# Setup, first norm and recurrence as one block; first mixture-of-experts layer, key norm and attention as another

## What is computed

```python
hn = rmsnorm(h, norm_mix_w[0])                       # layer 0: gated linear recurrence
q, f, i, g = split(hn @ w_in)
fg = lb + (1 - lb) * sigmoid(f); o, s = gla_chunked(silu(q), 1 - fg, i, log(fg), s0)
h = h + (rmsnorm(o, gnorm_w) * silu(g)) @ w_o
h = h + hier_moe(rmsnorm(h, norm_ffn_w[0]))          # 16 experts, 2 per token
kv = rmsnorm(h, kv_norm_w) @ w_kv                    # shared keys and values
hn = rmsnorm(h, norm_mix_w[1]); q = hn @ b_w_q       # layer 1: differential attention
h = h + (rmsnorm(attn(q, kv, cache), subln_w) * (1 - lam_init)) @ b_w_o
h = h + hier_moe(rmsnorm(h, norm_ffn_w[1])); y = rmsnorm(h, final_norm_w)
```

## Time and profile before

| | |
|---|---|
| median of three runs | 1624.22 us (1623.5 to 1628.1) |
| the profiled execution | 1626.92 us, its span 1625.2 us |
| PE busy | 1337.0 us (82%) |
| DVE busy | 745.8 us (46%) |
| ACT busy | 391.1 us (24%) |
| POOL busy | 168.7 us (10%) |
| granted PE clock, mean | 0.909 |

### The profile page before, as it was taken

One profiled execution on the slowest core, in us unless ns is written; L12 is line 12 of the kernel. 1 busy time (PEld: TensorE's weight loads), 2 busy tenths in 40 slices (PEclk: granted clock), 3 DMA queues, 4 the chain that ended last, 5 costly groups with the idle time before them and its releaser, 6 DMA issues. The chain is left out here.

```text
span 1625.2 us, 29095 instructions
## 1 busy us (share of the span) xinstructions
PE 1337.0 (82%) x11207; PEld 763.4 (47%) x11207; DVE 745.8 (46%) x1890; ACT 391.1 (24%) x1064; POOL 168.7 (10%) x242
## 2 busy tenths in 40 slices
PE   3999999988799998925999985877788589999880
PEld 2445555555456655513454542443444145765440
DVE  4315665656665311124110644787787166421115
ACT  2023443443110211103011022344444111121111
POOL 1002332332001000020000001001000001100002
PEclk9999999998898999966999988899898889799995
DMA  6141433123614999940132759999999761699924
GB/s 211 52 136 42 134 102 126 57 67 119 231 58 184 328 352 342 306 148 23 52 107 96 288 174 401 380 406 383 382 403 357 271 246 55 248 381 352 333 57 165
DMA packets 132156, 347.56 MB, mean 214 GB/s; under 512 B 22012, under 2 KB 51887, under 8 KB 123824
## 3 DMA queue, kind: packets, MB, share of 16 engines
q1 hardware_dynamic: 115652, 315.21, 53.7%
q0 software_dynamic: 4992, 17.83, 3.1%
q10 hardware_dynamic: 11372, 12.62, 2.5%
HBM read 302.09 MB, written 43.52 MB: 213 GB/s over the span
## 5 line engine op out<-in xcount | busy, mean ns | idle before, releaser
L404 PE MATMUL bank<-wring,xT 128*128 128x512 f32 x512 | 227.8, 602 | 5.0 <-PEq L359 4.4
L404 PEld LDWEIGHTS bank<-wring,xT 128*128 128x128 f32 x512 | 96.9, 192 | 124.6 <-issue 123.2
L785 PE MATMUL bank<-xT,wring 128*128 128x512 f32 x256 | 115.6, 609 | 10.2 <-DVE hgrn_g L621 10.2
L1313 PE MATMUL bank<-wring,xT 128*128 128x512 f32 x256 | 120.4, 624 | 2.0 <-DVE xT L1233 2.0
L2310 DVE STREAM_TRANSPOSE wring<-wring 128x1024 f32<-128x1024 f32 x64 | 77.2, 1227 | 41.8 <-DMA wring<-cache_k 41.5
L2310 DVE STREAM_TRANSPOSE attn_q_xT<-attn_q_xT 128x1024 f32<-128x1024 f32 x64 | 77.0, 1227 | 32.1 <-DMA attn_q_xT<-cache_k 31.8
L785 PEld LDWEIGHTS bank<-xT,wring 128*128 128x128 f32 x256 | 49.0, 194 | 73.3 <-issue 59.8
L1313 PEld LDWEIGHTS bank<-wring,xT 128*128 128x128 f32 x256 | 49.8, 201 | 60.1 <-issue 60.0
L695 DVE COPY_PREDICATED gla_att<-level_masks,bank 128x512 f32<-128x512 int32 x48 | 35.1, 731 | 61.3 <-PE bank L805 61.3
L1946 PE MATMUL bank<-attn_q_xT,wring 128*128 128x512 f32 x128 | 56.9, 597 | 0.0
L805 PE MATMUL bank<-gla_qe,gla_ke 128*128 128x128 f32 x384 | 51.8, 293 | 0.0
(11 more groups left out here) (426 smaller groups left out, 2329.7 us busy)
## 6 DMA issues: line engine op xcount, KB each, us to landing
wring<-cache_k SPq DMA_DIRECT2D x64, 512.0 KB, 7.1
attn_q_xT<-cache_k SPq DMA_DIRECT2D x64, 512.0 KB, 8.0
xT<-cache_v SPq DMA_DIRECT2D x60, 512.0 KB, 7.6
wring<-cache_v SPq DMA_DIRECT2D x56, 512.0 KB, 6.1
moe_wd<-moe_w_down SPq DMA_DIRECT2D x20, 1024.0 KB, 13.5
wring<-moe_w_gate SPq DMA_DIRECT2D x18, 1024.0 KB, 11.2
wring<-moe_w_up SPq DMA_DIRECT2D x18, 1024.0 KB, 14.1
wring<-a_w_in SPq DMA_DIRECT2D x16, 1024.0 KB, 8.6
```

Source lines behind the costliest of these rows:

```text
L404: last = nc.tensor.matmul(bank[:, :], xT[:, c, cols(t)], w[:, c, :], start=(c == 0), stop=(c == DC - 1))
L785: last = nc.tensor.matmul(bank[:, :], lhsT, k.xT[:, c, 0:SEQ], start=(c == 0), stop=(c == DC - 1))
L1313: last = nc.tensor.matmul(bank[:, :], k.xT[:, c, cols(t)], w[:, c, :], start=(c == 0), stop=(c == DC - 1))
```

## The change

The setup, the mix0 norm and the recurrence form one block; layer 0's output projection, experts, combination, the mix1 norm, projections and attention form another; layer 1's experts and the final combination form a third. Three blocks stand where there were nine.

In the first, SP issues the first three weight tiles right behind the tokens, without the waits for the small weights. ACT loads the column weights first, then the row weights. The norm goes by tile with `root` and `scale`; PE turns tiles 0 and 1, and then turns tile t + 2 behind value unit (0, t). DVE's clearing is spread between its copies. The lambda scalar is made later.

In the second, POOL waits for one semaphore (`finished`) that PE raises when all stores have landed, and gathers into ten buffers; `add` waits for both gathers of a tile; DVE adds, scales and turns out tile by tile, and PE projects both halves of the keys of tile t (four banks) as soon as its transposed tile is out. The second sample query goes from head 1 to head 4, and the spread of the sample queries from head 2 to head 6. The last expert's narrow stores are issued by SP and not by ACT, and the loop over extra blocks lies inside one `If(more > 0)`. In the third block the same holds, with six gather buffers for four. A small table load for the square root (`load_table`) stands ahead of the norms. Slot numbers and gates move to tiles that outlive the layer.

```diff
-            sp.wait_ge(columns_in, 16 * len(by_feature))
-            sp.wait_ge(rows_in, 16 * 6)
-            for i in range(2):
-                k.load_weights(sp, column_halves(a["a_w_in"][0], 2 * D + i * HB))
-            k.load_weights(sp, head_pair_halves(a, 0))
-            sp.wait_ge(tokens_in, 16 * NT)
...
+    def sync(self, sp):
+        k, a = self.k, self.a
+        for t in range(PT):
+            sp.dma_start(k.h[:, t, :], a["x_prompt"][0, t * P:(t + 1) * P, :]).then_inc(self.tokens_in[t], 16)
+        sp.dma_start(k.h[0:SMP, PT, :], a["x_sample"].rearrange("b t d -> (b t) d")).then_inc(self.tokens_in[PT], 16)
+        for i in range(2):
+            k.load_weights(sp, column_halves(a["a_w_in"][0], 2 * D + i * HB))
+        k.load_weights(sp, head_pair_halves(a, 0))
...
+    def scalar(self, act):
+        k, a = self.k, self.a
+        for i, w in enumerate(self.by_feature):
+            act.dma_start(self.weight_rows[i * DC:(i + 1) * DC, :], w.rearrange("(c p) -> c p", p=P)).then_inc(self.columns_in, 16)
+        act.dma_start(k.rowbuf[:, 0:P], a["a_gnorm_w"]).then_inc(self.rows_in, 16)
+        act.dma_start(k.rowbuf[:, P:2 * P], a["b_subln_w"]).then_inc(self.rows_in, 16)
+        for i, w in enumerate((a["b_lambda_q1"], a["b_lambda_k1"], a["b_lambda_q2"], a["b_lambda_k2"])):
+            act.dma_start(self.lam[:, i, :], w).then_inc(self.rows_in, 16)
...
+    def spread_rows(self, pe):
+        k, nc = self.k, self.nc
+        pe.wait_ge(self.rows_in, 16 * 6)
+        nc.tensor.matmul(k.ps[7][:, 0:2 * P], k.ones[0:1, :], k.rowbuf[:, 0:2 * P], start=True, stop=True).then_inc(self.spread, 1)
...
+                setup.scalar(act)
+                norm.root(act, 0)
+                for t in range(NT):
+                    if t + 1 < NT:
+                        if t + 1 == PT:
+                            act.wait_ge(setup.padded, 1)
+                        norm.root(act, t + 1)
+                    if t == 0:
+                        act.wait_ge(setup.out, 1)
+                    norm.out_second(act, t)
+                setup.lambda_exponentials(act)
...
+                setup.pad_rows(dve)
+                norm.scale(dve, ch, 0)
+                setup.lambda_products(dve)
+                setup.columns(dve)
+                dve.wait_ge(setup.out, 1)
+                norm.out_first(dve, 0)
+                norm.scale(dve, ch, 1)
+                norm.out_first(dve, 1)
+                norm.scale(dve, ch, 2)
+                setup.row_gains(dve)
+                norm.scale(dve, ch, 3)
+                norm.out_first(dve, 2)
+                norm.scale(dve, ch, 4)
+                value_out(0, 0)
+                norm.out_first(dve, 3)
+                nc.vector.memset(below[:, :, :], 0.0).then_inc(zero_made, 1)
+                value_out(0, 1)
+                norm.out_first(dve, 4)
+                bounds()
+                setup.lambda_sum(dve)
+                value_out(0, 2)
+                clear_level(0)
+                value_out(0, 3)
+                clear_level(1)
+                value_out(0, 4)
+                clear_level(2)
...
+                pe.wait_ge(setup.ident_made, 1)
+                norm.turn(pe, 0)
+                setup.turn_columns(pe)
+                norm.turn(pe, 1)
+                setup.spread_rows(pe)
+                w = k.take_weights(pe)
+                for t in range(NT):
+                    pe.wait_ge(norm.out_v, t + 1)
+                    pe.wait_ge(norm.out_a, t + 1)
+                    by_token(("v", 0, t), w)
+                    if t + 2 < NT:
+                        norm.turn(pe, t + 2)
+                k.w_done.append((proj_done, units[("v", 0, NT - 1)][0]))
+                w = k.take_weights(pe)
+                for t in range(NT):
+                    by_token(("v", 1, t), w)
+                    if t == 0:
+                        setup.spread_lambda(pe)
+                k.w_done.append((proj_done, units[("v", 1, NT - 1)][0]))
...
+        self.store_narrow(sp, E - 1, (E - 1) % NB, (E - 1) * CAP)
...
-        with sp.Fori(0, MORE) as i:
-            with sp.If(i < more):
+        with sp.If(more > 0):
+            with sp.Fori(0, MORE) as i:
...
-        pe.wait_ge(y_out[0], more * (16 * STORES) + 16 * STORES * loads_before(NB, 0))
+            pe.wait_ge(y_out[0], 16 * STORES * (loads_before(NB, 0) + MORE))
+        pe.wait_ge(y_out[0], 16 * STORES * loads_before(NB, 0))
         pe.wait_ge(y_out[1], 16 * STORES * loads_before(NB, 1))
...
+    def gpsimd(self, pool):
+        pool.wait_ge(self.finished, 1)
+        B = len(self.rows_in)
+        for n in range(TOPK * NT):
+            t, j = n // TOPK, n % TOPK
+            if n >= B:
+                pool.wait_ge(self.added, n - B + 1)
+            pool.indirect_dma_start(self.rows_in[n % B][0:rows(t), :], None, self.slots_y,
+                                    bass.IndirectOffsetOnAxis(ap=self.k.slot_i[0:rows(t), j, t:t + 1], axis=0))\
+                .then_inc(self.landed[n % B // TOPK], 16)
...
+    def add(self, dve, t):
+        k, B = self.k, len(self.rows_in)
+        for j in range(TOPK):
+            n = TOPK * t + j
+            if j == 0:
+                dve.wait_ge(self.landed[n % B // TOPK], 16 * TOPK * (n // B + 1))
+            if n:
+                dve.wait_ge(self.added, n)
+            part = k.h[0:rows(t), t, :]
+            self.nc.vector.scalar_tensor_tensor(out=part, in0=self.rows_in[n % B][0:rows(t), :], scalar=k.gates[0:rows(t), j, t:t + 1],
+                                                in1=part, op0=ALU.mult, op1=ALU.add).then_inc(self.added, 1)
...
+        k.w_done += [(self.k_done, 2 * NT - 1), (self.k_done, 2 * NT)]
+        self.norm.turn(pe, 0)
+        for n, (i, t) in enumerate(self.k_units):
+            if i == 0:
+                pe.wait_ge(self.norm.out_v, 2 * t + 1)
+                pe.wait_ge(self.norm.out_a, 2 * t + 1)
+            if n >= 4:
+                pe.wait_ge(self.k_out, n - 3)
+            project_tokens(nc, k.ps[n % 4], self.kv_xT, w[i], t).then_inc(self.k_done, 1)
+            if i == 0 and t + 1 < NT:
+                self.norm.turn(pe, t + 1)
...
+            if h == 4:
+                w.append(k.take_weights(pe))
+            if h % 4 == 0:
+                sample_q(h // 4, w[h // 4])
+            if h == 0:
+                pe.wait_ge(self.k_out, 2 * NT)
...
-            if h == 2:
+            if h == 6:
...
+        sp.wait_ge(self.combine.added, TOPK * NT)
...
+        def tile(t):
+            add(dve, t)
+            norm.scale(dve, ch, t)
+        tile(0)
+        norm.out_first(dve, 0)
+        tile(1)
+        tile(2)
+        norm.out_first(dve, 1)
+        key_out(0)
+        tile(3)
+        key_out(1)
+        norm.out_first(dve, 2)
+        key_out(2)
+        tile(4)
+        key_out(3)
+        norm.out_first(dve, 3)
+        key_out(4)
+        key_out(5)
+        norm.out_first(dve, 4)
+        for n in range(6, 2 * NT):
+            key_out(n)
...
+    def norm_scalar(self, act):
+        norm = self.norm
+        norm.load_table(act)
+        norm.root(act, 0)
+        norm.out_second(act, 0)
+        norm.root(act, 1)
+        for t in range(1, NT):
+            if t + 1 < NT:
+                norm.root(act, t + 1)
+            norm.out_second(act, t)
...
+                ffn.vector(dve)
+                ch = Chain(dve, k.order["vector"], k.order_n["vector"])
+                proj.combine_and_keys(dve, ch)
...
+            rows_in = [tile[:, t, :] for tile in (g, v) for t in range(NT)]
...
+                rows_in = [qo[:, t, :] for t in range(PT)] + [xs[:, PT, :], xs[:, PT - 1, :]]
```

528 lines of the change are left out of this document (251 added, 277 removed).

## The result

The changed kernel takes 1572.89 us (median of four runs, 1572.28 to 1574.52) against 1623.86 us before (four runs, 1617.76 to 1628.1); the ratio is 0.9687, with a 95% interval of 0.9657 to 0.9717. The forecast was 1577. Measured twice more, the same pair gave 0.9713 (0.9672 to 0.9754) and 0.9740 (0.9716 to 0.9764). Over all fourteen runs the changed kernel has a median of 1575.2 and a mean of 1575.9.

What follows compares the result with a forecast made beforehand. PE, busy 82% of the span, was taken as the bound, so gains come from its idle stretches: 13.7 + 30.2 + 3.7 = 47.6 us off 1626.9 gives 1579.3, less 2.7 for the median, 1577; range 1566 to 1596.

Steps and rivals of the forecast that it cites:

- Opening: Start to first value unit and the turns behind it: first unit at 20.5 instead of 36.70, 13.7 us gained in all.
- Middle: Layer 0's experts to layer 1's queries: first key unit 34.4 us earlier, 4.2 given back by turns, 30.2 us gained.
- End: Final combination after layer 1's experts: first gather 5.0 us earlier, 1.3 given back waiting for both gathers, 3.7 us gained.
- The bound of 29.5 for the first unit: Opening's worst case: small loads end behind tokens and three weight tiles, near 24; first value unit at 29.5, gain 4.7.
- the narrowest place: Keys of layer 1, tile 1: PE's second tile ready at about 737, PE comes at 740, 3 us of slack.
- the loop and the barrier: Layer 0's experts' end: the first gather came only at 714.41 because all engines went through both.
- (a): Opening: the small loads end late, costing up to 9 us, so 1586; chance 0.13.
- (b): Keys of layer 1: DVE's chain sets the pace, 10 us lost, 1587, or 1596 with (a); chance 0.12, with or without (a).
- (d): Keys of layer 1: PE's clock stays low through all keys, 56 us lost, 1633; chance 0.03.
- (e): First key unit still waits until all tiles are scaled; only barriers go, about 20 us gained, 1604; chance 0.05.
- (c): All three stretches gain more, 17.2 + 33 + 6 = 56 us, 1568; chance 0.12.
- a sign of an error: Recurrence or attention: the prediction would be wrong if either changed its own length.

Runs made afterwards that it cites:

- keys_after_norm: Changed kernel, but PE turns all five tiles of layer 1's norm before the first key unit; 1597.4 us against 1575.05 for the changed kernel on the same chip.
- the last experiment: Changed kernel with early square-root table load, tiles 0 and 1 squared before row loads, later row-weight spreading, separate first-row semaphore; 1569.11 us against 1577.41.

## Why the prediction was right, point by point

**The sum.** Opening 13.7 forecast, 13.9 measured at the recurrence's end (mean of nine traces against three). Middle 30.2 forecast; from the last product to the sample query it was 117.1 and 116.7 before and 85.8, 84.7 and 88.1 changed, so 30.7. End 3.7 forecast; from the last product to the last store's issue it was 43.5 and 44.0 before and 40.3, 39.6 and 39.9 changed, so 3.8. Together 48.4 for 47.6. The first median of the changed kernel, 1572.89, lies 4 below the forecast, and the mean of all fourteen runs, 1575.9, lies 1 below it.

**The opening's terms.** The first value unit came at 19.4 and not at 20.5, because the second turn was ready 0.6 earlier and the spreading followed at once. Two of the three turns between the value units took 1.04 each and the small one 0.68, for 1.04 and 0.65. That the sum comes out at 13.9 for 13.7 is partly luck: the first unit gained 17.1 and not 16.2, and the recurrence behind it gave back 3.2 and not 2.5 (381.2 in the mean of nine, 378.0 before). Up to the features the changed kernel's first trace gave back 2.6, as forecast; the rest lies in the recurrence, which no term covers. The bound of 29.5 for the first unit was too low by the prediction's own steps: from the column weights (12.8) to the first unit (20.5) it has 7.7 us, and 24 + 7.7 is 31.7. No run came near it. That the weight tile is no limit was right, with less room than I thought: in at 15.5, not 13 to 14.

**The middle's terms.** Additions 6.5 us behind the first gather (6.7 forecast), key units to sample query 64.8 (64.6 by the sum of 60.4 and 4.2), no stop of PE for DVE. At the narrowest place, tile 1, DVE had written its half for the keys at 716.4 and PE's unit began at 721.5, a slack of 5.1 us and not 3. The gather itself came 5.1 behind the product (6.3 forecast). The cause behind that term I had not separated. I laid the old 13.2 us at "the loop and the barrier" in one breath; the runs give 7.3 to the loop, and what was left for barrier and stores is 0.7. That PE passes the loop's end during the landing was right, though its one branch alone takes 3.8 us there.

**The end's terms.** The first gather came 4.5 to 5.0 us earlier behind the product (11.2 before; 6.7, 6.2 and 6.5 changed), for 5.0; the wait for both gathers gave back about 0.9 of it (32.6 to 33.5), for 1.3.

**The rivals.** (a) fell: no small load was waited for, neither as changed nor when issued later. (b) fell: 4.6 us of cover in each of tiles 2 to 4. (d) fell: the clock was back at 1.00 behind the first key unit and stayed there. The Trainium skill (TensorE: Matmul & The Clock Gate, HAM oscillation) ties a return to the lower level to idle gaps in PE's work; PE had none from 713.70 to 768.83, and the clock was 1.00 there, so the trace agrees with the page. (e) did not happen; made on purpose in keys_after_norm it gives 1597.4; I had priced it at 1604, a gain of 20 to 23, where the run has 27 against its kernel before (1624.4). (c) did not come either: 48 us were gained and not its 56, since the opening had the second turn in its way and the end gave 3.8 and not 6 (its time of 1568 is also the low end, which the forecast then put at 1566).

**Not foreseen** was the spread of single stretches: 6 to 7 us in each experts' stretch and 10 in attention, with PE's work the same. I had called a change of length of the recurrence a sign of an error. It was none: 377.6 to 383.0 us in traces with the new opening, where I expected 378 + 2.5.

## What to carry to other kernels

Joining blocks gained little by itself here, 0.7 to 1.6 us a barrier (measured with the loop still ahead of it); the gain comes from what the joining allows, which is feeding the bound engine by the first tile while the others are still being prepared (24 of 31 us). Look for short runtime loops whose bodies are never entered: a pass costs the same whether its body is one instruction or a hundred, apart from the first jump over the long one, and one branch around the loop removes the passes but not that jump. When a stage starts earlier, compare the same stage in several traces of both kernels before its length is put down to the change, above all where its DMA share is near 1.

## What the runs showed of the hardware that I had not expected

- A pass of a register loop whose body is not entered costs PE's sequencer 0.76 us, over a body of one instruction as over a whole expert. The first jump over a long stretch of code costs more, 3.3 to 3.9 us in layer 0 of every trace, the next ones over the same code about 0.22.
- The same 2.87 us of idle time on PE is followed by a granted clock of 0.91 over 20 us in one execution and 1.00 in another. Such spells go with a spread of 5 us in a recurrence whose waits are the same.
- Six loads of 0.2 to 0.5 KB issued on ACT while SP was queueing 6 MB of weights were in within 8.5 us of the last one's issue, and PE did not wait for them.
- A square root's table, loaded while the tokens were in flight, also served the squares: two table loads of 1.28 us became one, and it left the chain (the last experiment).
